# Fetching the stored product back behind the last exponentials, and splitting the output weights behind the last values

## What is computed

```python
y_a = chunked_spatial_gating(gelu(z_a), ...)            # first branch
y_b = dilated_mixture_attention(q, k, v)                # second branch, 3 groups of 4 heads
gates = sigmoid(gate_logits.reshape(b, s, 2, D_MODEL))
merged = gates[:, :, 0] * (y_a @ w_branch_a) + gates[:, :, 1] * (y_b @ w_branch_b)
x = x + merged @ w_out
```

## Time and profile before

| | us |
|---|---|
| runs | 1957.14, 1951.63, 1957.41 (median 1957.14) |
| the profiled execution, its own time | 1954.66 |
| its span, first to last instruction | 1952.8 |
| TensorE busy | 1844.9 (94% of the span) |
| VectorE busy | 983.0 (50%) |
| ScalarE busy | 654.9 (34%) |
| GpSimd busy | 85.1 (4%) |
| mean granted clock of TensorE | 0.975 of full speed |

### The profile page before, as it was taken

One profiled execution on the slowest core, in us unless ns is written; L12 is line 12 of the kernel. 1 busy time (PEld: TensorE's weight loads), 2 busy tenths in 40 slices (PEclk: granted clock), 3 DMA queues, 4 the chain that ended last, 5 costly groups with the idle time before them and its releaser, 6 DMA issues.

```text
span 1952.8 us, 22760 instructions
## 1 busy us (share of the span) xinstructions
PE 1844.9 (94%) x9397; PEld 1336.6 (68%) x9403; DVE 983.0 (50%) x1620; ACT 654.9 (34%) x1126; POOL 85.1 (4%) x70
## 2 busy tenths in 40 slices
PE   5999999999999699999999899998998899999998
PEld 4877887788878434343443278897777788888886
DVE  4887887833542322231322153638384556536643
ACT  4455554432232301020110053424555333213233
POOL 0200001000000000000000000003030200000000
PEclk9999999999999699999999999999999999999999
DMA  9342423452351499999999942272121422233221
GB/s 323 127 130 77 141 76 98 130 173 87 103 231 68 167 415 421 421 422 421 420 421 422 409 141 81 70 220 65 44 84 38 156 71 85 89 119 105 73 89 43
DMA packets 174521, 355.10 MB, mean 182 GB/s; under 512 B 7154, under 2 KB 144466, under 8 KB 149074
## 3 DMA queue, kind: packets, MB, share of 16 engines
q1 hardware_dynamic: 170672, 338.85, 47.1%
q10 hardware_dynamic: 3458, 14.50, 2.1%
q0 software_dynamic: 288, 0.30, 0.1%
HBM read 345.53 MB, written 8.39 MB: 181 GB/s over the span
## 4 chain that ended last, share of the span: by engine, by line
PE 80%; DVE 9%; DMA 4%; ACT 4%; issue 2%; POOL 1%; SPq 0%; ACTq 0%; DVEq 0%
PE ps L492 77%; PE ps L495 3%; DMA rx<-in_w_exp_down 1%; DMA rx<-in_w_exp_up 1%; POOL X L2813 1%; DMA md<-in_w_mod 1%; DVE wsq1l L1896 1%; DVE wsp0l L1896 1%; DVE X L1905 1%; DVE small L2141 1%; ACT M L1250 1%; DVE k2l L1896 0%; ACT KR L1250 0%; DMA M2b<-m_spill 0%; DVE tb L1896 0%
## 5 line engine op out<-in xcount | busy, mean ns | idle before, releaser
L492 PE MATMUL ps<-H,wsq1h 128*128 128x512 f32 x640 | 200.4, 394 | 4.7 <-DVE wsq1l L1896 2.7
L492 PE MATMUL ps<-H,wsq0h 128*128 128x512 f32 x608 | 191.2, 396 | 0.2 <-DVE wsq0l L1896 0.2
L492 PE MATMUL ps<-rx,XE 128*64 128x512 f32 x752 | 178.5, 606 | 2.8 <-DMA rx<-in_w_exp_up 2.2
L492 PE MATMUL ps<-H,wsp1h 128*128 128x512 f32 x544 | 172.6, 399 | 1.4 <-DVE wsp1l L1896 1.4
L492 PEld LDWEIGHTS ps<-H,wsq1h 128*128 128x128 f32 x640 | 120.2, 190 | 30.6 <-issue 6.0
L492 PEld LDWEIGHTS ps<-H,wsq0h 128*128 128x128 f32 x608 | 114.5, 190 | 25.6 <-issue 2.3
L492 PE MATMUL ps<-H,wsq1l 128*128 128x512 f32 x320 | 125.3, 391 | 0.0
L492 PE MATMUL ps<-H,wsp0h 128*128 128x512 f32 x368 | 121.4, 408 | 2.1 <-ACT H L1250 2.1
L1896 DVE TENSOR_TENSOR wsq1l<-ring,wsq1h 128x1024 fp32r<-128x1024 f32 (+2 forms) x72 | 82.8, 1190 | 77.9 <-ACT wsq1h L1250 77.9
L492 PE MATMUL ps<-H,wsq0l 128*128 128x512 f32 x304 | 119.1, 392 | 0.0
L492 PEld LDWEIGHTS ps<-rx,XE 128*64 128x64 f32 x752 | 49.7, 138 | 95.9 <-issue 84.8
(11 more groups left out here) (378 smaller groups left out, 3458.6 us busy)
## 6 DMA issues: line engine op xcount, KB each, us to landing
rx<-in_w_exp_gate SPq DMA_DIRECT2D x49, 1024.0 KB, 17.2
rx<-in_w_exp_down SPq DMA_DIRECT2D x46, 1024.0 KB, 20.7
rx<-in_w_exp_up SPq DMA_DIRECT2D x45, 1024.0 KB, 19.1
ring<-in_w_in SPq DMA_DIRECT2D x37, 1024.0 KB, 5.5
ring<-in_w_up SPq DMA_DIRECT2D x20, 1024.0 KB, 5.2
ring<-in_w_exp_up SPq DMA_DIRECT2D x19, 1024.0 KB, 20.5
ring<-in_w_mod SPq DMA_DIRECT2D x18, 1024.0 KB, 7.3
ring<-in_w_exp_down SPq DMA_DIRECT2D x18, 1024.0 KB, 19.0
```

The costliest lines, as they stand in the source:

```text
L492: return pe.e.matmul(o, l, r, start=start, stop=stop, skip_group_check=True)
```

## The change

Two things move; nothing is added or taken away.

1. ScalarE issues the fetch of the stored product into `M3`, with its two semaphore waits, right behind the exponentials of (1, 3) inside the loop, instead of at the end of the attention.
2. On ScalarE and VectorE the split of slab ("wo2", 0) goes behind the values of (1, 3) instead of ahead of them.

```diff
@@ scalar @@
             for r in range(4):
                 soft2(jj, r)
+                if (jj, r) == (1, 3):
+                    ac_.wait_ge(S["m_out"], "m")
+                    ac_.wait_ge(S["pe_score"], (1, 3, 1, 2))
+                    load("m_back", "m", M3[:, :], m_d)
                 next(more, None)
                 next(more, None)
                 if turned:
...
         hi(slabs["bb"])
         values2(*turned)
         turn2(*scored)
+        values2(*scored)
         hi(slabs["wo2", 0])
-        values2(*scored)
-        ac_.wait_ge(S["m_out"], "m")
-        ac_.wait_ge(S["pe_score"], (1, 3, 1, 2))
-        load("m_back", "m", M3[:, :], m_d)
```

## The result

The changed kernel takes 1947.12 us, median of 12 runs (1943.09 to 1952.21), beside 1953.68 us for the kernel before, median of 12 runs on the same chip (1948.63 to 1957.41). The ratio is 0.9969, 95% interval 0.9956 to 0.9982: about 0.3% faster. By that interval the gain is 3.5 to 8.6 us.

The account below looks back on a forecast made before the run. VectorE's eight pairs were taken to bound the stretch, their start set by the fetch. Part 1 gives 3.6 us, part 2 nothing, clock loss unchanged: 1956.6 less 3.6 is 1953.0 us, range 1948.5 to 1957.3.

Parts of the forecast that it names:

- Against which time: Choice of starting time: 1956.6 us, between the profiled execution's 1954.66 and the median 1957.14, giving 1953.0.
- the better clock case: Rival on TensorE's clock behind its gap: no low-clock loss, gain 5.2 us, time 1951.4; chance 9%.
- the sum: VectorE's first sum starts 3.64 us earlier, at 1514.82; block 7's product and TensorE's output product follow; gain 3.6 us.
- Part 1: Fetch on ScalarE's queue: issued by 1501.6 at no cost, landed at 1509.6, 5 us ahead of need; gives 3.6 us.
- Part 2: Split behind the values: TensorE's 2.05 us idle falls by 1.92, but without a receiver; nothing gained at the end.
- The bound: Stretch ahead of the output product: VectorE's eight pairs bound it, and the fetch sets when they start.
- met GpSimd at a worse moment: Rival on shared ports: VectorE's sums arrive just behind GpSimd's start and wait 1.27 us; price +2.1, 1958.7; chance 4%.
- The clock cost as much as before: TensorE behind its gap ahead of the output product: half-speed loss taken as unchanged, 1.60 us.
- The clock costs nothing: Rival: no low-clock loss for TensorE behind the gap; 1956.6 - 5.2 = 1951.4 us; chance 9%.
- The change did what it says: Opposite of a rival where the fetch is held or lands later than 1514.8, VectorE waiting as before: 1956.6; chance 7%.

Follow-up runs that it names:

- again: The changed kernel timed a second time without an edit: 1948.85 us beside 1952.45 for the kernel before, ratio 0.9982.
- again2: The changed kernel timed a third time without an edit: 1949.37 us beside 1953.94 for the kernel before, ratio 0.9978.
- split_alone: The kernel before with only the split of slab (wo2, 0) moved behind the values, fetch at its old place: 1956.74 us, ratio 1.0010.
- fetch_alone: The kernel before with only the fetch moved behind the exponentials, split still ahead of the values: 1947.92 us, ratio 0.9978.
- banks_before: The kernel before with only the PSUM banks of the first output product turned by one: 1947.74 us, ratio 0.9984.
- null: The kernel before, unedited, timed as if it were a change: 1952.86 us, ratio 1.0003.
- mid_fetch: The kernel before with the fetch issued behind the values of (1, 2), split unmoved: 1950.04 us, ratio 0.9995.
- banks_again: The changed kernel with the first output product's PSUM banks turned by one, timed a second time: 1941.28 us beside 1950.65 for the kernel before, ratio 0.9957.

## Why the prediction was wrong in its number and right in its mechanism

**The step that failed is "Against which time".** It took 1956.6 as the start, "nearer to the median", from three runs between 1951.63 and 1957.41. The kernel before has a median of 1953.68 in 12 runs on the chip of the comparison, and of 1952.45, 1953.94 and 1950.65 on three more occasions. The start was 2.9 us too high. 1953.68 - 3.6 = 1950.1 would have been in the range. The range shares in the step: its low end, 1948.5, stands above the 1948.0 that its own sentence works out, and the lowest run less the 5.2 of the better clock case would have been 1946.4. The profiled execution, at 1954.66, was the better witness: it was a fourth run, and it lay in the middle. The rest of the miss, 3.0 us, is the difference between 6.6 in the first comparison and the 3.6 of the sum; between the medians of again and again2 the difference was 3.6 and 4.6. The first interval, 3.5 to 8.6 us, holds the forecast gain; what the excess is made of stays open.

**Part 1** went as reckoned: the issue hidden, the product landed before it was wanted, the pairs straight behind the low split. I had put the issue behind the second exponential, 8.7 us ahead of the end of the values; it came during the first, 10.4 ahead. The next copy is that of the values of (1, 1), not (1, 2) as I wrote; it waits for TensorE all the same. With nothing beside it the fetch took 7.7 us from issue to landing, against the 8.02 that I used.

**Part 2** was put at nothing at the end, with TensorE's 1.92 us lost for want of a receiver. The runs bear this out: split_alone turned the 2.05 us gap into a longer one behind "bb". The 0.4 us between fetch_alone and the changed kernel come from VectorE's first product, at 3.92 behind the values there and 3.62 here. I had the first product 3.80 behind the end of the values (1514.10 - 1510.30), and it came at 1505.90 - 1502.28 = 3.62, since the high split starts 0.19 us behind the start of the copy and not behind its end. In all the sum was off by 0.15 us.

**The bound.** I named VectorE's eight pairs. The gap was predicted at 4.1 and measured at 3.99, the stretch at 3.64 shorter and measured at 3.79. But the pairs bound TensorE only through one bank, and my text passed over that as a given. It changes nothing in the forecast, and it is what an engineer should have seen: banks_before gains more in its stretch than the change does (6.0 against 3.8 us), though not by its runs (4.0 against 5.1).

**The rivals.** The sums beside GpSimd took 1.04 to 1.07 us, as before, so none met GpSimd at a worse moment. GpSimd's low parts in the changed kernel, all eight and then the first two:

```profile
L2814 POOL TENSOR_TENSOR MH<-X,MH x8: 1279/1720/1747, 1508.2 to 1519.9; 128x512 fp32r<-128x512 f32 x8
...
1508.15 1.64 POOL L2814 TENSOR_TENSOR MH<-X,MH 128x512 fp32r<-128x512 f32 x1 [61.40 <-ACT MH L1250]
1509.76 1.74 POOL L2814 TENSOR_TENSOR MH<-X,MH 128x512 fp32r<-128x512 f32 x1
```

The third sum started at 1509.28, while the first low part ran until 1509.79, and ended at 1510.35. Less the 0.69 us that a sum takes alone, it was held until 1509.66, so nearly to the end of the low part. The second low part ended at 1511.50; less the 1.28 of the shortest one, it was held until 1510.22, so nearly to the end of the sum. Each waited for what was left of the other's instruction. The rule of the Trainium skill, "SBUF — State Buffer", section "SBUF: two separate sides", that whoever starts first holds the shared ports for its whole instruction, agrees with these rows within some 0.15 us. The rival priced a sum that arrives just behind GpSimd's start and waits the full 1.27; the pattern moved as a whole, and the sums waited 0.35 to 0.38.

The clock cost as much as before, 3.4 us at half speed and so about 1.7 lost against 1.60. "The clock costs nothing" came true only in the kernels with turned banks, where there is no gap ahead of the output product. The change did what it says.

## What to carry to other kernels

Take the time that a forecast starts from with the scatter of its runs, and let the profiled execution count as one of them: here the start was wrong by 2.9 us and the sum by 0.15. When an engine waits for "the last of eight", ask whether it needs the last, or only stands on its buffer: turning the rotation of the banks by one line gave 4.5 us more by the runs (5.4 by the profiles) on top of a change that gave 4 to 5. And a difference at a place that the change cannot reach is to be tested by more profiles of both kernels before it is explained.

## What the runs showed of the hardware

- The same gap of TensorE does not drop the clock in each execution. Ahead of 304 us TensorE idles 2.62 us in the first profile of the kernel before and 2.63 in that of the changed one; the first then ran at 1.2 GHz and the second at 2.4. Of the 14 profiles 6 were low there: before, null, null2, split_alone, mid_fetch and banks_again, so with the late, the middle and the early place of the fetch.
- TensorE at half speed can cost next to nothing where another engine sets the end: in null it was at 0.54 behind the `ybl` gap, and the stretch was at most 0.3 us longer for it (19.38 beside 19.10 to 19.28).
- The fetch of 2 MB took 7.7 to 7.8 us from issue to landing with nothing beside it, and also in mid_fetch, where SyncE's fetch of 1 MB was issued 5.9 us behind it. It took 8.0 to 8.6 where SyncE's was issued 2.5 to 3.6 us behind it.
- ScalarE's queue issued the DMA ahead of work that stands before it in the program: at 1491.90, during the first exponential (1491.77 to 1492.67) and before the second started at 1492.66.
- VectorE's sum and GpSimd's low part hold each other up for the rest of the instruction that runs: a sum took 1.04 to 1.07 us beside one and 0.69 alone.
